# The second MLP product by Strassen's scheme, in two passes, with two blocks' norms under the second pass

## Chip, cores and metric

The program runs on one core of one Trainium2 chip. The metric is the time of one execution in microseconds (us) on the device, the median of the runs made. An engine is named here by what it does: TensorE multiplies (PE in the rows; PEld is its loading of the stationary operand), VectorE is DVE, ScalarE is ACT, GpSimd is POOL, and SyncE (SP) issues most of the loads.

## What is computed

Two transformer-like blocks run one after the other on 512 tokens of width 1024, all in float32. The part around the change is the end of the first block and the start of the second:

```python
hn = rms_norm(x, norm2_w[l])
x = x + jnp.square(jax.nn.relu(hn @ mlp_w1[l])) @ mlp_w2[l]
...
return rms_norm(x, final_norm_w)
...
h = _rmsnorm(x, mix_norm_g[i])
z = h @ w_in[i]
u_f = z[..., :FOURIER_WIDTH]
u_s = z[..., FOURIER_WIDTH:FOURIER_WIDTH + SSM_WIDTH]
```

`mlp_w2` is 4096 x 1024. Behind it come a Fourier mix, a state-space mix, gates, an output product, a router and 64 experts with a hidden width of 512, whose weights are all read from HBM.

## The kernel before

Each engine has one program written out in order; semaphores join them. Tokens are four blocks of 128 (`i`). The eight PSUM banks of 512 columns are handed out by the helper `T` (class `Psum`): `full` counts a bank's finished tiles, `free` its emptied ones. `any_bank` hands the banks out in a ring. Weights go through four SBUF slots of 2 MB, `WR[0]` to `WR[3]`; the list `plan` says which weight takes which slot, and `load` in the program of SyncE waits, before it issues a transfer, until the last user of that slot is done. Transfers are issued strictly in the order of that program.

- The first MLP product (`mlp_in`) makes 32 tiles `("m1", m)` of 128 features by 512 tokens, eight matmuls each. ScalarE takes the ReLU (L1257), GpSimd squares (L2275), and the result is `HT`, 32 chunks `k` of 128 features by 512 tokens; semaphore `ht` counts them.
- Woven between these tiles stands the preparation of the state-space matrices in eight turns `c` (`ssm`): VectorE and GpSimd make outer products, TensorE transposes them (L664, L667) and multiplies small tiles (`zb`, L678, L684), ScalarE writes the results to DRAM (`mbr_d`, `mbi_d`, `mcr_d`, `mci_d`, `z_d`; semaphores `st0`, `st1`). On VectorE a table of powers (`Ep`, L1466 and L1869) follows.
- The second MLP product: `acc` holds 8 banks, block `i` by half `nh` of the 1024 outputs. In step `s_` one 2 MB piece of `m2` (four chunks `k`) is multiplied into all eight banks, 32 matmuls of 128x128 by 128x512 (L703; the profile counts two instructions for each float32 matmul). The last step goes bank by bank (L720).
- Behind it the residual is added (`add_m2`, L1882), the block gets its final norm (`final_norm`, L1887 and L1892, with ScalarE's squares L1069 and root L1319), then the norm of the second model (`mix_norm`, L1897, L1902, root L1327), TensorE transposes it (`mix_norm` on TensorE, L389), VectorE and ScalarE move it to `H` (`turn_out`, L1485, L1075), and `z2` (eight tiles, weights in two pieces) is multiplied, its first four tiles as two halves of 256 tokens (`half_tile`, L401), the others whole (`dense`, L382).
- `z2` tiles 0 to 3 go through DRAM (`u_d`) into `U` in another order; only then can TensorE start the state products `("v", ri, g8)` (L749, 64 columns each) with `mbr_d`, then `mbi_d`, read back. The Fourier tiles (L760), `yf` (L382), `within` (L778, needs `z_d` read back by L2448) and `borders` (L800, needs VectorE's scan: semaphore `sp`, four and then eight) follow. 
- Later the gates, the output product, the router and the experts follow; the experts' weights pass through nine slots.

## Time and profile before

| | |
|---|---|
| median of 3 runs | 2427.59 us (2423.2 to 2429.49) |
| span of the profiled execution | 2424.5 us |
| TensorE busy | 2204.2 us, 91% |
| TensorE's weight loading busy | 1011.7 us |
| VectorE, ScalarE, GpSimd busy | 607.9, 320.6, 212.6 us |
| mean granted TensorE clock | 0.972 of full speed |
| second MLP product, L703 and L720 | 835.12 to 1055.96 us |
| expert weights | from 1447.48 us on without a pause, about 425 GB/s |

The profiled execution has no time of its own beside its span; the span lies inside the range of the runs, 3.1 us under their median, so what a sum takes from the span is taken from the median too. An engine's share of busy time says nothing of one stage: a stage is read from its own rows. 1.00 of granted clock is 2.4 GHz, 0.50 is 1.2 GHz.

### The profile page before, as it was taken

How to read it: one execution, taken by the hardware profiler on the slowest of the kernel's cores; microseconds unless marked ns; L12 is line 12 of the kernel's file. 1: busy time of each engine (PE TensorE's matmuls, PEld its weight loads, DVE VectorE, ACT ScalarE, POOL GpSimd, SP SyncE). 2: the span in 40 equal slices, each digit the busy share in tenths (PEclk: the TensorE clock that was granted, in tenths of full speed). 3: DMA queues.
4: the chain of work that ended last, by engine and by line, in shares of the span. 5: the costliest groups of instructions: out<-in, count | busy, mean ns of one | idle time of the engine just before them, and what ended most of it. 6: DMA issues, size and time to landing. Idle time of an engine off the chain costs nothing.

```text
span 2424.5 us, 20330 instructions
## 1 busy us (share of the span) xinstructions
PE 2204.2 (91%) x8260; PEld 1011.7 (42%) x8260; DVE 607.9 (25%) x1295; ACT 320.6 (13%) x645; POOL 212.6 (9%) x192
## 2 busy tenths in 40 slices
PE   8999999999999999999999999978877888877776
PEld 5554444445444444466644463333322233322332
DVE  2146545301633220044621151110111111111114
ACT  2015324201111100021110120000000000000001
POOL 0001111010234200000000000000000000000001
PEclk9999999999999999998999999998999999999998
DMA  7201010321232321219523349999999999999995
GB/s 275 87 35 70 35 70 18 139 104 72 102 108 89 143 78 69 78 49 161 178 104 130 147 167 413 427 426 426 426 426 426 426 426 426 425 425 422 424 422 219
DMA packets 69759, 551.39 MB, mean 227 GB/s; under 512 B 21656, under 2 KB 26392, under 8 KB 37600
## 3 DMA queue, kind: packets, MB, share of 16 engines
q1 hardware_dynamic: 42384, 514.44, 52.2%
q10 hardware_dynamic: 17200, 23.23, 3.2%
q0 software_dynamic: 10080, 12.38, 1.5%
q8 instruction: 67, 1.10, 0.2%
q14 instruction: 28, 0.23, 0.0%
HBM read 542.86 MB, written 35.68 MB: 239 GB/s over the span
## 4 chain that ended last, share of the span: by engine, by line
PE 70%; DMA 25%; DVE 2%; ACT 1%; issue 1%; DVEq 0%; POOL 0%; ACTq 0%; SPq 0%; POOLq 0%
PE ps L382 25%; DMA sb<-in_eu 13%; DMA sb<-in_eg 9%; PE ps L1019 9%; PE ps L458 8%; PE ps L703 8%; PE ps L1051 4%; DMA sb<-in_ed 3%; PE ps L401 3%; PE ps L633 2%; PE ps L867 2%; PE ps L546 1%; PE ps L579 1%; PE ps L573 1%; PE ps L800 1%
## 5 line engine op out<-in xcount | busy, mean ns | idle before, releaser
L382 PE MATMUL ps<-sb 128*128 128x512 f32 (+2 forms) x1504 | 599.8, 558 | 2.3 <-issue 2.3
L1019 PE MATMUL ps<-sb 128*64 128x512 f32 x2048 | 487.0, 631 | 114.5 <-DMA sb<-in_eu 81.7
L382 PEld LDWEIGHTS ps<-sb 128*128 128x128 f32 x1504 | 273.7, 190 | 308.0 <-issue 304.7
L1019 PEld LDWEIGHTS ps<-sb 128*64 128x64 f32 x2048 | 175.6, 145 | 405.2 <-issue 405.1
L1051 PE MATMUL ps<-sb 128*64 128x512 f32 x992 | 227.8, 613 | 27.0 <-ACT sb L1442 17.3
L458 PE MATMUL ps<-sb 128*128 128x512 f32 x512 | 236.1, 600 | 0.1
L703 PE MATMUL ps<-sb 128*128 128x512 f32 x448 | 192.5, 592 | 0.7 <-ACT sb L1257 0.7
L1466 DVE TENSOR_TENSOR sb<-sb 128x512 f32<-128x512 f32 (+9 forms) x293 | 114.7, 410 | 114.3 <-PE ps L667 66.2
L1051 PEld LDWEIGHTS ps<-sb 128*64 128x64 f32 x992 | 73.3, 141 | 160.1 <-issue 135.4
L458 PEld LDWEIGHTS ps<-sb 128*128 128x128 f32 x512 | 91.2, 190 | 100.0 <-issue 98.2
L703 PEld LDWEIGHTS ps<-sb 128*128 128x128 f32 x448 | 85.0, 190 | 107.6 <-issue 107.6
L2360 POOL DMA_INDIRECT y_d<-sb x31 | 31.2, 1007 | 854.2 <-PE ps L1003 748.7
L2219 DVE SCALAR_TENSOR_TENSOR sb<-sb,ps 128x512 f32<-128x512 f32 x32 | 22.1, 690 | 301.8 <-PE ps L1019 301.8
L1081 ACT ACTIVATE sb<-ps 128x512 f32<-128x512 f32 (+3 forms) x100 | 52.8, 536 | 240.4 <-PE ps L382 77.7
L2214 DVE SCALAR_TENSOR_TENSOR sb<-sb,ps 128x512 f32<-128x512 f32 x32 | 22.1, 690 | 245.3 <-ACT sb L1438 245.3
L2264 POOL TENSOR_TENSOR sb<-sb 128x256 f32<-128x256 f32 (+3 forms) x32 | 41.6, 1300 | 371.0 <-DVE sb L1682 370.9
L1490 DVE COPY sb<-ps 128x512 f32<-128x512 f32 (+6 forms) x53 | 34.4, 650 | 145.7 <-PE ps L382 89.8
L1442 ACT ACTIVATE sb<-ps 128x512 f32<-128x512 f32 x32 | 19.2, 598 | 376.0 <-PE ps L1026 376.0
L401 PE MATMUL ps<-sb 128*128 128x256 f32 x256 | 61.7, 403 | 6.3 <-DVE sb L1485 3.5
L2209 DVE TENSOR_TENSOR sb<-ps,sb 128x512 f32<-128x512 f32 x64 | 41.4, 687 | 102.6 <-PE ps L1003 101.8
L2229 DVE COPY sb<-ps 128x512 f32<-128x512 f32 x31 | 21.5, 693 | 176.6 <-PE ps L1051 176.6
L867 PE MATMUL ps<-sb 128*128 128x512 f32 x128 | 58.4, 598 | 1.6 <-DVE sb L2008 1.6
(288 smaller groups left out, 1474.7 us busy)
## 6 DMA issues: line engine op xcount, KB each, us to landing
sb<-in_eg SPq DMA_DIRECT2D x64, 2048.0 KB, 32.8
sb<-in_eu SPq DMA_DIRECT2D x63, 2048.0 KB, 33.9
sb<-in_ed SPq DMA_DIRECT2D x63, 2048.0 KB, 33.0
sb<-in_m SPq DMA_DIRECT2D x16, 2048.0 KB, 7.3
sb<-in_mg SPq DMA_DIRECT2D x8, 1536.0 KB, 6.6
sb<-in_winF SPq DMA_DIRECT2D x5, 2048.0 KB, 7.3
sb<-in_mgg SPq DMA_DIRECT2D x4, 2048.0 KB, 7.9
sb<-in_wo SPq DMA_DIRECT2D x4, 2048.0 KB, 7.4
```

The source lines that it names most:

```text
L382: ins = pe.matmul(out, lhsT, rhs, start=k == 0, stop=k == len(pieces) - 1)
L401: ins = pe.matmul(T.ap(*tile)[:, t], lhsT, rhs[:, t], start=k == 0, stop=k == 7)
L458: ins = pe.matmul(o, lhsT, rhs, start=k == 0, stop=k == 7)
L633: ins = pe.matmul(o, MG1[:, k, 128 * i:128 * i + 128], wo[nh][:, k, :], start=k == 0, stop=k == 7)
L703: ins = pe.matmul(acc[2 * i + nh], HT[:, k, 128 * i:128 * i + 128], w[:, q, 512 * nh:512 * nh + 512], start=k == 0, stop=False)
L867: ins = pe.matmul(T.ap(*name), MG2[:, k, 128 * i:128 * i + 128], wo[nh][:, k, :], start=k == 0, stop=k == 7)
L1019: ins = pe.matmul(o[64 * e:64 * e + 64, :], x[:, k, 64 * e:64 * e + 64], weight(2 * mat + e)[:, 512 * k:512 * k + 512], start=k == 0, stop ...
L1051: ins = pe.matmul(o[64 * e:64 * e + 64, :], aT[:, k, 64 * e:64 * e + 64], weight(4 + e)[:, d:d + 512], start=k == 0, stop=k == 3)
L1081: act.activation(dst, T.ap(*name) if src is None else src, ACT.Copy).then_inc(T.s(*name), 1)
L1466: return own(dve.tensor_tensor(o, a, b, op))
L2209: dve.tensor_tensor(XT[:, 4 * hf:4 * hf + 4, :], table.ap("xt", q, hf).rearrange("p (a b) -> p a b", a=4), bc(ck("gx")[:, 4 * hf:4 * hf + ...
L2264: pool.tensor_tensor(pr, pr, bc(ST[u % 4][:, 2:4], 2, nk), ALU.mult).then_inc(S("prob"), 1)
```

## The change

The product by `m2` is done in two passes (`turn`), each for two token blocks. In a pass, a step takes the same 2 MB piece as before, seen as 2 x 2 blocks (pairs of feature chunks, even and odd, by halves of the outputs), and one level of Strassen's scheme in Winograd's form makes seven products of two matmuls each where the plain scheme for two token blocks has eight. So `m2` is read twice: 16 loads in place of 8. VectorE makes four sums of weights (`t`, 1024 elements per partition) and four of activations (`a`, 256 elements) per step (`block_sums`), double-buffered in `TW` and `SW`: the first step's weight sums lie where the table `Ep` comes later, those of odd steps in `WR[3]`, those of even steps in `H`. Seven banks accumulate the products `f`; the eighth (`bank_t`) holds transposes. At the end of a pass `block_results` combines the seven products with the residual.

The norms of blocks 0 and 1 stand in VectorE's and ScalarE's programs between the sums of the second pass, and their transposes stand on TensorE between the products of step 15. The table of powers is a generator whose pieces stand between the sums of steps 2 to 6. The last `zb` tile stands ahead of the last `m1` tile. Of `z2` five tiles, not four, are done as halves. Its pieces take other slots, so that `mbr_d` and `mbi_d` are read back after `z2` at earlier places.

```diff
+        TW = [view(zone, 20480, 4, 2, 512), view(WR[3], 0, 4, 2, 512)]
+        TW += [shaped(H.rearrange("p a b -> p (a b)"), 8, 512).rearrange("p (a c) b -> p a c b", c=2)]
+        SW = [[view(zone, 2048 + 1024 * q, 8, 128) for q in range(2)], [HT[:, 8 * q:8 * q + 8, 0:128] for q in range(2)]]
+        UW = [[view(zone, 512 * q, 2, 256) for q in range(3)], [HT[:, 16 + 2 * q:18 + 2 * q, 0:256] for q in range(3)]]
...
-        plan += [(("m1", g), (0, 2, 1)[g % 3]) for g in range(8)] + [(("m2", g), g % 3) for g in range(8)]
-        plan += [(("z2", 0), 3), (("z2", 1), 0), (("dft", 0), 1), (("mbr", 0), 3), (("mbi", 0), 0), (("z", 0), 3),
+        plan += [(("m1", g), (0, 2, 1)[g % 3]) for g in range(8)] + [(("m2", g), (1, 0, 2)[g % 3]) for g in range(16)]
+        plan += [(("z2", 0), 0), (("z2", 1), 2), (("dft", 0), 1), (("mbr", 0), 3), (("mbi", 0), 0), (("z", 0), 3),
...
+        def step_done(n):
+            return T.full("m2", n // 8, 6) if n % 8 == 7 else (S("m2w"), n + 1 - n // 8)
+
+        def sums_of(n):
+            t = TW[0] if n == 0 else TW[1] if n % 2 else TW[2]
+            s_ = SW[n // 8][n % 2]
+            return [t[:, q] for q in range(4)], [s_[:, 2 * q:2 * q + 2, :] for q in range(4)]
...
+            base = ring[0]
+            bank_t = (base + 7) % 8
+            for n in range(16):
+                turn, s_ = n // 8, n % 8
+                tsum, ssum = sums_of(n)
+                w = view(slot("m2", n), 0, 2, 2, 2, 512)
+                lo, hi = slice(256 * turn, 256 * turn + 128), slice(256 * turn + 128, 256 * turn + 256)
+                pe.wait_ge(*loaded("m2", n))
+                if turn == 0:
+                    pe.wait_ge(S("ht"), 4 * s_ + 4)
+                even, odd = [4 * s_, 4 * s_ + 2], [4 * s_ + 1, 4 * s_ + 3]
+                factors = [
+                    ([HT[:, k, lo] for k in even], [w[:, j, 0, 0] for j in range(2)]),
+                    ([HT[:, k, lo] for k in odd], [w[:, j, 1, 0] for j in range(2)]),
+                    ([ssum[1][:, j] for j in range(2)], [tsum[1][:, j] for j in range(2)]),
+                    ([ssum[2][:, j] for j in range(2)], [tsum[2][:, j] for j in range(2)]),
+                    ([ssum[0][:, j] for j in range(2)], [tsum[0][:, j] for j in range(2)]),
+                    ([ssum[3][:, j] for j in range(2)], [w[:, j, 1, 1] for j in range(2)]),
+                    ([HT[:, k, hi] for k in odd], [tsum[3][:, j] for j in range(2)]),
+                ]
+                for f, (a, b) in enumerate(factors):
+                    if s_ == 0:
+                        open_tile(pe, ("m2", turn, f), (base + f) % 8)
+                    if f == 2:
+                        pe.wait_ge(S("m2s"), n + 1)
+                    for j in range(2):
+                        ins = pe.matmul(T.ap("m2", turn, f), a[j], b[j], start=s_ == 0 and j == 0, stop=s_ == 7 and j == 1)
+                    if s_ == 7:
+                        ins.then_inc(T.f("m2", turn, f), 1)
+                    elif f == 6:
+                        ins.then_inc(S("m2w"), 1)
+                    if n == 15 and f in (0, 2, 3, 5):
+                        i, h = divmod((0, 2, 3, 5).index(f), 2)
+                        pe.wait_ge(S("xn"), 4 + i + 1)
+                        turned_half(2, i, h, XN, bank_t)
+                W.ended[("m2", n)] = n
...
+            half_tile(2, ("z2", 0), "z2", 0, 0, bank_t)
+            half_tile(2, ("z2", 1), "z2", 1, 0, base % 8)
+            half_tile(2, ("z2", 2), "z2", 2, 0, (base + 1) % 8)
+            mix_norm(2, 3)
+            half_tile(2, ("z2", 3), "z2", 3, 0, (base + 2) % 8)
+            mix_norm(3, 5)
+            pe.wait_ge(*loaded("z2", 1))
+            half_tile(2, ("z2", 4), "z2", 4, 0, (base + 3) % 8)
+            for m in range(5):
                 half_tile(2, ("z2", m), "z2", m, 1)
-            for m in range(4, 8):
+            ring[0] = base + 4
+            for m in range(5, 8):
                 dense(("z2", m), "z2", m, any_bank())
...
+            first_product(0)
             sums(0)
-            root_a(0)
-            sum_b(0)
             sums(1)
-            root_b(0)
-            root_a(1)
-            sum_b(1)
+            for i in range(2):
+                root_a(i)
+                sum_b(i)
+            for i in range(2):
+                root_b(i)
+            first_product(1)
+            turn_out(2, 0, sm("mix"))
+            turn_out(2, 1, sm("mix"))
...
-                        yield
+                        if c < 7 or way:
+                            yield
...
+                    if q == 5:
+                        yield
...
+            def block_sums(n):
+                turn, s_ = n // 8, n % 8
+                t, a = sums_of(n)
+                w = view(slot("m2", n), 0, 2, 2, 2, 512)
+                b11, b12, b21, b22 = w[:, :, 0, 0], w[:, :, 0, 1], w[:, :, 1, 0], w[:, :, 1, 1]
+                lo, hi = slice(256 * turn, 256 * turn + 128), slice(256 * turn + 128, 256 * turn + 256)
+                h = HT[:, 4 * s_:4 * s_ + 4, :].rearrange("p (j q) b -> p j q b", q=2)
+                a11, a12, a21, a22 = h[:, :, 0, lo], h[:, :, 1, lo], h[:, :, 0, hi], h[:, :, 1, hi]
+                dve.wait_ge(*loaded("m2", n))
+                if n == 0:
+                    dve.wait_ge(*T.full("mb", 7, 1))
+                elif n == 1:
+                    dve.wait_ge(S("st0"), 512)
+                    dve.wait_ge(S("st1"), 512)
+                elif n == 2:
+                    dve.wait_ge(*T.full("m1", 31))
+                    dve.wait_ge(*step_done(0))
                 else:
-                    after(own(ins))
-                    cmul(pw2[q % 2], pw, pw)
-                    pw = pw2[q % 2]
-
-
-            def add_m2(i):
-                for nh in range(2):
-                    xs = X[:, i, 512 * nh:512 * nh + 512]
-                    dve.wait_ge(*T.full("m2", i, nh))
-                    dve.scalar_tensor_tensor(xs, T.ap("m2", i, nh), norm_r[1][:, i:i + 1], xs, ALU.mult, ALU.add).then_inc(T.s("m2", i, nh), 1)
+                    dve.wait_ge(*step_done(n - 2))
+                if turn == 0:
+                    dve.wait_ge(S("ht"), 4 * s_ + 4)
+                t1 = tt(t[0], b12, b11, ALU.subtract)
+                if n == 0:
+                    dve.wait_ge(*T.full("zb", 7, 1))
+                s1 = tt(a[0], a21, a22, ALU.add)
+                after(t1)
+                t2 = tt(t[1], b22, t[0], ALU.subtract)
+                after(s1)
+                s2 = tt(a[1], a[0], a11, ALU.subtract)
+                tt(t[2], b22, b12, ALU.subtract)
+                tt(a[2], a11, a21, ALU.subtract)
+                after(t2)
+                tt(t[3], b21, t[1], ALU.subtract)
+                after(s2)
+                dve.tensor_tensor(a[3], a12, a[1], ALU.subtract).then_inc(S("m2s"), 1)
...
+                dve.wait_ge(*T.free("m2", turn, 0))
+                after(own(add(x00, r0, p1)))
+                add(x00, r0, product(1)).then_inc(T.s("m2", turn, 1), 1)
+                dve.tensor_tensor(u2, product(2), p1, ALU.add).then_inc(T.s("m2", turn, 2), 1)
+                dve.wait_ge(*T.free("m2", turn, 2))
+                x01_u2 = own(add(x01, r0, u2))
+                dve.tensor_tensor(u3, product(3), u2, ALU.add).then_inc(T.s("m2", turn, 3), 1)
+                yield
+                dve.wait_ge(*T.free("m2", turn, 3))
+                x10_u3 = own(add(x10, r1, u3))
+                x11_u3 = own(add(x11, r1, u3))
+                after(x01_u2)
+                x01_p5 = own(add(x01, r0, product(4)))
+                after(x11_u3)
+                add(x11, r1, product(4)).then_inc(T.s("m2", turn, 4), 1)
+                after(x01_p5)
+                add(x01, r0, product(5)).then_inc(T.s("m2", turn, 5), 1)
+                after(x10_u3)
+                add(x10, r1, product(6)).then_inc(T.s("m2", turn, 6), 1)
...
+            for n in range(9):
+                block_sums(n)
+                if 2 <= n < 7:
+                    next(ep_steps, None)
+            for _ in ep_steps:
+                pass
+            for _ in block_results(0):
+                pass
...
+            block_sums(9)
+            for i in range(2):
+                block_sums(10 + i)
+                final_norm(i)
+            for i in range(2):
+                block_sums(12 + i)
+                mix_norm(i)
+            block_sums(14)
+            block_sums(15)
             turn_out(2, 0, sm("mix"))
+            results = block_results(1)
+            next(results)
+            turn_out(2, 1, sm("mix"))
+            for _ in results:
+                pass
             final_norm(2)
-            add_m2(3)
+            final_norm(3)
...
+            pool.wait_ge(*step_done(0))
...
-            for g in range(8):
-                load(("m2", g), A["m2"][:, 4096 * g:4096 * g + 4096])
-            sp.wait_ge(S("mg1"), 8)
-            sp.wait_ge(S("st0"), 512)
-            sp.wait_ge(S("st1"), 512)
+            for n in range(16):
+                load(("m2", n), A["m2"][:, 4096 * (n % 8):4096 * (n % 8) + 4096])
             for g in range(2):
                 fours("z2", g, 8)
             load(("dft", 0), A["dft"], 2048)
+            sp.wait_ge(S("st0"), 512)
+            sp.wait_ge(S("st1"), 512)
+            sp.wait_ge(*step_done(15))
```

How the order of instructions changes on TensorE at the start of the second product (bank semaphores `free`, `ht` of the activations, `m2s` of the sums, `w` of a slot's load). Before, the last small tiles of `ssm` (L678) stand between the last `m1` tile (L382) and the product, whose first instruction waits for all eight banks:

```order
L382 MATMUL ps<-sb 128x512 [waits free2]
L382 MATMUL ps<-sb 128x512 x7
L678 MATMUL ps<-sb 16x128 [waits free3]
L678 MATMUL ps<-sb 16x128 x7
L703 MATMUL ps<-sb 128x512 [waits free5,free6,free4,free7,free3,w0,free2,ht,free1,free0]
L703 MATMUL ps<-sb 128x512 x7
L703 MATMUL ps<-sb 128x512 [waits ht]
```

and now (L396 is the `m1` tile, L738 the new product):

```order
L698 MATMUL ps<-sb 16x128 [waits free2]
L698 MATMUL ps<-sb 16x128 x7
L396 MATMUL ps<-sb 128x512 [waits free3]
L396 MATMUL ps<-sb 128x512 x7
L738 MATMUL ps<-sb 128x512 [waits free4,ht,w1]
L738 MATMUL ps<-sb 128x512
L738 MATMUL ps<-sb 128x512 [waits free5]
L738 MATMUL ps<-sb 128x512
L738 MATMUL ps<-sb 128x512 [waits m2s,free6]
```

The product starts on one bank that was emptied long ago, and the first thing in a step that needs VectorE's sums is its fifth matmul.

On TensorE at the end of the product, before (L389 are transposes of normed blocks, semaphore `xn`; L401 the halves of `z2`):

```order
L389 MATMUL ps<-sb 128x128 [waits free2,xn]
L389 MATMUL ps<-sb 128x128 x3
L389 MATMUL ps<-sb 128x128 [waits free3]
L389 MATMUL ps<-sb 128x128 x3
L401 MATMUL ps<-sb 128x256 [waits free1,free2,free0,free3,w3]
L401 MATMUL ps<-sb 128x256 x7
L389 MATMUL ps<-sb 128x128 [waits free4,xn]
```

and now, from the last product of step 15 on (L410 are transposes, L421 the halves of `z2`):

```order
L738 MATMUL ps<-sb 128x512 x2
L421 MATMUL ps<-sb 128x256 [waits free3,w0]
L421 MATMUL ps<-sb 128x256 x7
L421 MATMUL ps<-sb 128x256 [waits free3,free4]
L421 MATMUL ps<-sb 128x256 x7
L421 MATMUL ps<-sb 128x256 [waits free3,free5]
L421 MATMUL ps<-sb 128x256 x7
L410 MATMUL ps<-sb 128x128 [waits free7,xn]
L410 MATMUL ps<-sb 128x128 x3
```

Three halves of `z2` now stand between the end of the product and the transposes of block 2, and one more ahead of those of block 3; before, the first half of `z2` waited for blocks 0 and 1 and stood right behind their transposes.

On VectorE behind the last turn of `ssm`, before, the powers come first:

```order
L1466 TENSOR_TENSOR sb<-sb 128x32 [waits ep_one,mcm]
L1466 TENSOR_TENSOR sb<-sb 128x32
L1466 TENSOR_TENSOR sb<-sb 128x32 [waits dve]
L1466 TENSOR_TENSOR sb<-sb 128x32
L1466 TENSOR_TENSOR sb<-sb 128x32 [waits dve]
```

and now the eight sums of step 0 stand there, then those of steps 1 and 2, before the powers begin:

```order
L1499 TENSOR_TENSOR sb<-sb 128x1024 [waits full7,ht,w1,mcm]
L1499 TENSOR_TENSOR sb<-sb 128x256 [waits full2]
L1499 TENSOR_TENSOR sb<-sb 128x1024 [waits dve]
L1499 TENSOR_TENSOR sb<-sb 128x256 [waits dve]
L1499 TENSOR_TENSOR sb<-sb 128x1024
L1499 TENSOR_TENSOR sb<-sb 128x256
L1499 TENSOR_TENSOR sb<-sb 128x1024 [waits dve]
L1951 TENSOR_TENSOR sb<-sb 128x256 [waits dve]
L1499 TENSOR_TENSOR sb<-sb 128x1024 [waits st1,ht,st0,w0]
```

`full2` is the last `zb` tile, which reads what the first activation sum overwrites.

## Rows read from the trace of the kernel before

**Rows 1.** The page: busy time, share of the span, instructions

```profile
PE 2204.2 (91%) x8260; PEld 1011.7 (42%) x8260; DVE 607.9 (25%) x1295; ACT 320.6 (13%) x645; POOL 212.6 (9%) x192
```

**Rows 2.** Timeline of TensorE: start, length, what, [idle before <- what ended it]

```profile
607.70 48.23 PE L382 MATMUL ps<-sb 128*128 128x512 f32 x112
...
835.12 192.50 PE L703 MATMUL ps<-sb 128*128 128x512 f32 x448 [0.66 <-ACT sb L1257]
1027.46 20.76 PE L720 MATMUL ps<-sb 128*128 128x512 f32 x48
...
1060.35 6.55 PE L401 MATMUL ps<-sb 128*128 128x256 f32 x16 [3.51 <-DVE sb L1485]
...
1075.39 17.43 PE L401 MATMUL ps<-sb 128*128 128x256 f32 x80
...
1120.13 7.25 PE L749 MATMUL ps<-sb 128*128 128x64 f32 x64
1128.41 11.58 PE L749 MATMUL ps<-sb 128*128 128x64 f32 x64 [1.03 <-DMA sb<-mbi_d]
1139.79 3.73 PE L760 MATMUL ps<-sb 128*128 128x128 f32 x16
...
1144.98 2.05 PE L760 MATMUL ps<-sb 128*128 128x128 f32 x16
...
1154.92 3.68 PE L778 MATMUL ps<-sb 128*128 128x64 f32 x32
...
1182.95 7.25 PE L800 MATMUL ps<-sb 128*128 128x64 f32 x64
```

**Rows 3.** Stretches: PE, PEld, DVE, ACT, POOL busy; PEclk, DMA share, GB/s

```profile
600.00:640.00 40.00, 40.00 (x113) 21.13 (x112) 30.40 (x127) 7.04 (x13) 6.27 (x6) 1.00 0.21 79
...
1060.00:1066.00 6.00, 5.65 (x13) 4.55 (x14) 2.30 (x8) 0.20 (x1) 0.00 (x0) 0.50 0.08 30
...
1120.00:1127.00 7.00, 7.00 (x64) 6.87 (x62) 3.99 (x6) 1.77 (x3) 5.57 (x4) 1.00 0.80 295
...
1131.00:1144.00 13.00, 13.00 (x62) 12.56 (x62) 10.67 (x11) 2.85 (x6) 0.29 (x2) 0.50 1.28 108
...
1450.00:2380.00 930.00, 760.04 (x3384) 290.83 (x3382) 108.31 (x179) 55.67 (x93) 60.73 (x60) 0.95 1.00 422
```

**Rows 4.** Timeline of VectorE

```profile
703.31 1.32 DVE L1466 TENSOR_TENSOR sb<-sb 128x512 f32<-128x512 f32 x1 [11.66 <-PE ps L667]
...
842.48 0.98 DVE L1466 TENSOR_TENSOR sb<-sb 128x32 f32<-128x32 f32 x5 [34.84 <-POOL sb L2309]
...
851.02 0.42 DVE L1869 TENSOR_TENSOR sb<-sb 128x256 f32<-128x256 f32 x1
...
863.08 1.23 DVE L1869 TENSOR_TENSOR sb<-sb 128x1024 f32<-128x1024 f32 x1
...
1036.07 0.21 DVE L1887 TENSOR_SCALAR sb<-sb 128x1 f32<-128x1 f32 x1 [0.79 <-ACT sb L1069]
...
1037.59 1.28 DVE L1892 SCALAR_TENSOR_TENSOR sb<-sb 128x1024 f32<-128x1024 f32 x1
...
1070.02 0.15 DVE L1897 TENSOR_SCALAR sb<-sb 128x1 f32<-128x1 f32 x1 [1.96 <-ACT sb L1069]
...
1071.48 0.75 DVE L1902 TENSOR_SCALAR sb<-sb 128x1024 f32<-128x1024 f32 x1
...
1176.97 1.21 DVE L1973 TENSOR_TENSOR sb<-sb 64x1008 f32<-64x1008 f32 x1
```

**Rows 5.** Transfers: issue on ScalarE's queue with its time, then counts, KB, us to landing

```profile
1104.07 5.57 ACTq L1363 DMA_DIRECT2D sb<-u_d  x8
...
sb<-in_m SPq DMA_DIRECT2D x16, 2048.0 KB, 7.3
...
sb<-z_d SPq DMA_DIRECT2D x8, 256.0 KB, 11.5
...
sb<-u_d ACTq DMA_DIRECT2D x8, 128.0 KB, 7.0
```

137 lines of the change are left out of this document (57 added, 80 removed).

## Prediction

> **What bounds the kernel now.** I read the page first: TensorE is busy for 91% of the span [rows 1]. Then its timeline around the change [rows 2], for its idle times and what ended them, and the same stretches with the granted clock [rows 3]. TensorE runs without a gap through the second product: 448 of its 512 instructions take 192.5 us, 0.430 each. Behind it stand two stalls. The first is 3.51 us ahead of the first `z2` half, which waits for the norms of the last blocks on VectorE. The second is 1.03 us in the state products, for `mbi_d`. Behind each the clock falls to 0.50: over 1060 to 1066, and over 1131 to 1144 [rows 3]. Later, from 1450 us on, the DMA share is 1.00 and the experts' weights set the pace [rows 3]. Their first buffers come free only through routing and the first experts, which stand behind all of this on TensorE; so what TensorE gains here moves the whole stream, and I count it in full.
>
> **What is removed.** (a) Strassen: 16 steps x 7 products x 2 matmuls = 224 matmuls against 256, so 64 of 512 instructions fewer, at 0.430: 27.5 us.
>
> (b) The product's first instruction waited 0.66 us for the bank of the last `m1` tile; now it takes a bank emptied earlier: 0.7 us.
>
> (c) The stall of 3.51 us ahead of `z2`, and the slow clock behind it. The first half tile took from 1060.35 to the transposes at about 1066.8, 6.4 us; five half tiles together took 17.43, 3.45 each from start to start [rows 2]. So 2.9 more, in all 6.4 us. The cover now: three halves of `z2`, 10.4 us, between the end of the product and block 2's transposes. VectorE must in that time add the last product (under 1 us), do the final norms of blocks 2 and 3 (from 1036.07 to 1038.87, 2.8 each) and the mix norm of block 2 (from 1070.02 to 1072.23, 2.2) [rows 4]: 8.6, and with the squares and roots of ScalarE that stand between them some 10, an estimate. Block 3's second norm has a further 1.0 (transposes) and 3.45, and needs 2.2 and two moves. Both fit with a few tenths to spare; I allow 0.5 for small waits.
>
> (d) `mbi_d` could be loaded only when the last `z2` tile was done. Now it takes the slot of the first piece of `z2` and starts after tile 3, more than 20 us earlier for a transfer of 8: the 1.03 us go. And the slow clock with them, I think: 64, 16, 8 and 16 instructions from 1128.41 to 1147.0 took 18.6 us; at the full clock 7.1 (as the 64 ahead of them) + 2.05 + 1.0 + 2.05 = 12.2 [rows 2], 6.4 less. In all 7.4 us.
>
> The clock term rests on this: the 64 state instructions at 1120 ran for 7 us with the clock at 1.00, and it fell only after the stall [rows 3]. "Activity releases the throttle" is how the Trainium skill has it (TensorE: Matmul & The Clock Gate, Part 1); by that rule (d) stands in full.
>
> **What is added, and what hides it.** (e) VectorE's sums, per step 4 of 1024 elements at 1.23 and 4 of 256 at 0.42: 6.6 us [rows 4]. TensorE's step lasts 28 x 0.430 = 12.0, and its first four matmuls, 3.4 us, need no sum. The sums of step n may start when step n-2 is done. The first piece of the powers (it ends ahead of the 128x256, so by 851.44) takes at most 9.0 from 842.48, all pieces 21.8 [rows 4]. So at the fullest place, counted from the end of step 0, the sums of step 2 end at 6.6, that piece at 15.6, the sums of step 3 at 22.2, and TensorE wants them at 24.0 + 3.4; five turns are 55 against 60. For step 0 the last `m1` tile (6.9 us) and the first four matmuls are the cover. Cost nothing; were there no cover, 105 us.
>
> (f) Does VectorE's traffic slow TensorE? At 607 to 655 us TensorE took 48.23 / 112 = 0.431 per instruction [rows 2], with VectorE 76% busy over 600 to 640 [rows 3]. Nothing; the bounds are 0 and 0.2% of 192 us.
>
> (g) Loads: 16 in place of 8, 7.3 us each [rows 5], one per 12.0 us. A load starts when its slot's step is done and its sums may start one step later, so 4.7 us are spare. Nothing.
>
> (h) `block_results(0)`: eleven operations of at most 0.75 behind the sums of step 8, done some 15 us after step 7 begins; the second pass wants bank `f` from 12.0 + 1.7 `f` on, and the banks come free in that order, bank 1 some 5 us ahead. Nothing. In step 15 the four transposes (no more of them than before) share one bank; each of its emptyings, about 1.1 us on ScalarE, lies under at least one product of 1.7.
>
> (i) Given back: TensorE arrives 7.4 us earlier, measured from the start of the state products, than two things that don't move with it. `z_d` is issued 7.25 us behind that start and moves 2.1 MB at the 108 GB/s of that stretch, 19.4 us [rows 3]: there at 26.7, while TensorE now wants it at 34.8 - 7.4 = 27.4 (1154.92 less 1120.13). It just fits. VectorE's scan ended at 1178.18 and was wanted at 1182.95 [rows 2, 4], 4.8 us spare; it starts behind a state tile that itself comes about 2 us earlier, so 4.8 + 2 - 7.4 = -0.6. I take 0.9 for both.
>
> Sum: 27.5 + 0.7 + 6.4 + 7.4 - 0.5 - 0.9 = 40.6 us. From the span, 2424.5 - 40.6 = 2383.9; as the median stands 3.1 above, 2387.0.
>
> **The rivals.**
> 1. The clock falls in the state products all the same. For it: their tiles are 64 columns wide, and at 1131 to 1144 it stayed low although TensorE never idled; it rose only with the wider work. Against it: the 7 us at 1.00 ahead [rows 3]. Another road to the same end: `U` comes late. Its eight reads were issued by 1109.6 and land in 7.0, by 1116.6; that is 23.8 us behind the end of `z2` tile 3 (1092.8). The cover was 27.3 and is now one half and three whole tiles, 3.45 + 3 x 6.9 = 24.1: 0.3 us spare by that bound. Then (d) is 1.0 and (i) is nothing: 27.5 + 0.7 + 6.4 + 1.0 - 0.5 = 35.1, 2392.5. Chance 0.25.
> 2. The norms come late after all, TensorE waits again ahead of block 2's transposes, and the clock falls behind it. (c) is lost and a stall of up to 3.5 may stand in its place: 34.2 less, 2393.4; with rival 1, 2399. For it: the margin is under 1 us on an estimate of ScalarE's share. Chance 0.11.
> 3. On the other side: VectorE's sums become the bound. For it: an addition of 512 elements took 1.32 us with GpSimd beside it [rows 4], twice as much per element as the 1024 in 1.23. If strided operands in four dimensions cost the same without GpSimd, a step is 13.3, above 12.0, and the powers come on top: 16 x 1.3 + 22 = 43 us lost, 2430. It decides from 12.0 + 40.6 / 16 = 14.5 us a step. Against it: GpSimd stands idle here but for the last squares. Chance 0.03. The Trainium skill (SBUF — State Buffer, SBUF: two separate sides) makes that 1.32 an exclusive lock on a port pair that only VectorE and GpSimd share; by that rule only the sums of step 0 can double, and the sum stays as it is.
> 4. Switching banks costs time: seven banks in turn, each tile of two matmuls, and TensorE idles a little at every change until the clock drops. At the half clock the product would take up to 192 us more, some 2579. Against it: the old product changes its bank at every matmul and still keeps 0.430 [rows 2]. Chance 0.01. The rule is the Trainium skill's (TensorE: Matmul & The Clock Gate, A second HAM failure mode: psum-queue depth-cycling).
> 5. The experts' stream doesn't move, because something other than TensorE's path opens it: 2427.6. Nothing in the rows names such a thing. Chance 0.02.
>
> **How the numbers follow.** My forecast has 0.58; its own range is 2383 to 2391 (waits in (c) and (i) between 0 and 4). The likeliest is 2387.0. Rivals 1 and 2 reach to 2399; the range 2381 to 2397 leaves out their joint case and the others. A difference of 0.3% (7.3 us) is about what measurements of this kernel can tell. Faster: 0.58 + 0.25 + 0.11 = 0.94; within 0.3%: rival 5 and a hundredth of rival 3, which ends near the old time, 0.03; slower: the rest of rival 3 and rival 4, 0.03.
>
> **What would show it.** The product from its first to its last matmul near 192.4 us plus 2 of transposes, with no idle time above a few tenths inside, VectorE busy for about 6.6 us in every 12. No wait ahead of `z2` above 0.5, no clock of 0.50 there. `mbi_d` issued right behind tile 3 of `z2`; 128 state instructions in 14.5 us. If the clock falls there, rival 1. If `m2s` ends waits in the product, rival 3. A wait of TensorE for `xn`, rival 2. What would make all of it wrong is an expert stream that starts no earlier.

## The result, and the profile after

| | before | changed |
|---|---|---|
| median of 4 runs each | 2428.54 us (2423.20 to 2433.60) | 2393.62 us (2388.03 to 2406.47) |
| ratio | | 0.9872, 95% interval 0.9854 to 0.9891 |
| span of the profiled execution | 2424.5 us | 2386.2 us |
| VectorE busy | 607.9 us | 712.7 us |

The changed kernel is 1.3% faster; I had forecast 2387.0. By the ratio it stands at 2397.5 where before stands at 2428.5, and 2397.5 is also the median of the 16 executions made of it on three occasions. They lie between 2386 and 2409, twice as far apart as those of the kernel before (2422 to 2434), and where that spread comes from is half of the story. (The ratio is not that of the two medians alone; where a text below compares two kernels "by the ratios", it compares each one's ratio to the kernel before.)

The page of the changed kernel, the line that answers to [rows 1]:

```profile
PE 2179.7 (91%) x8212; PEld 998.7 (42%) x8212; DVE 712.7 (30%) x1437; ACT 321.8 (13%) x647; POOL 216.8 (9%) x192
```

Its timeline of TensorE (start, length, line, tile, idle time before it and what ended that), from the product to `borders`. L738 is the product, L410 transposes, L421 the halves of `z2`, L396 whole tiles, L776 the state products, L787 and L793 the Fourier tiles, L805 `within`, L827 `borders`; it answers to [rows 2]:

```profile
830.79 182.13 PE L738 MATMUL ps<-sb 128*128 128x512 f32 x424
...
1024.81 10.52 PE L421 MATMUL ps<-sb 128*128 128x256 f32 x48
1035.17 1.04 PE L410 MATMUL ps<-sb 128*128 128x128 f32 x8
...
1061.10 20.76 PE L396 MATMUL ps<-sb 128*128 128x512 f32 x48
1081.70 14.43 PE L776 MATMUL ps<-sb 128*128 128x64 f32 x128
1095.96 2.00 PE L787 MATMUL ps<-sb 128*128 128x128 f32 x16
...
1101.86 7.11 PE L396 MATMUL ps<-sb 128*128 128x512 f32 x16 [0.95 <-issue]
1112.42 7.09 PE L805 MATMUL ps<-sb 128*128 128x64 f32 x32 [3.45 <-DMA sb<-z_d]
1119.30 4.96 PE L396 MATMUL ps<-sb 128*128 128x512 f32 x8
1124.10 3.68 PE L805 MATMUL ps<-sb 128*128 128x64 f32 x32
1127.62 3.65 PE L396 MATMUL ps<-sb 128*128 128x512 f32 x8
...
1145.12 7.25 PE L827 MATMUL ps<-sb 128*128 128x64 f32 x64
```

Three things are to be seen. The product has no idle time, nor has anything behind it for 270 us: the stalls of 3.51 and 1.03 us of [rows 2] are gone. All 128 state instructions run in 14.43 us, at the full clock. And a new stall stands ahead of `within`: 3.45 us for `z_d`, which before was there in time. Behind it 32 instructions take 7.09 us, where the next 32 take 3.68, and 8 take 4.96, where the next 8 take 3.65. So the half clock costs 3.4 + 1.3 = 4.7 more.

The windows of this kernel (PE, PEld, DVE, ACT, POOL busy; PEclk, DMA share, GB/s), the answer to [rows 3]:

```profile
843.00:883.00 40.00, 40.00 (x94) 17.68 (x93) 34.92 (x79) 0.00 (x0) 0.21 (x2) 1.00 0.49 184
1025.00:1035.00 10.00, 10.00 (x48) 8.79 (x48) 6.76 (x22) 4.57 (x14) 0.00 (x0) 1.00 0.81 315
1083.00:1097.00 14.00, 14.00 (x127) 14.00 (x127) 8.56 (x12) 4.73 (x8) 5.41 (x4) 1.00 0.57 55
1113.00:1121.00 8.00, 8.00 (x33) 7.08 (x33) 7.87 (x8) 0.00 (x0) 0.00 (x0) 0.50 0.36 146
```

VectorE, the neighbour of [rows 4] here, has a step's seven sums of L1499 and the eighth of L1951 in 6.0 us, and the norms of the last blocks just ahead of the transposes at 1035.17 and 1039.50:

```profile
843.17 5.63 DVE L1499 TENSOR_TENSOR sb<-sb 128x1024 f32<-128x1024 f32 x7 [8.29 <-PE ps L738]
848.73 0.42 DVE L1951 TENSOR_TENSOR sb<-sb 128x256 f32<-128x256 f32 x1
...
1033.54 0.75 DVE L2013 TENSOR_SCALAR sb<-sb 128x1024 f32<-128x1024 f32 x1
...
1038.55 0.75 DVE L2013 TENSOR_SCALAR sb<-sb 128x1024 f32<-128x1024 f32 x1
```

The useful balance is by stage. From the first instruction of the product to the second `borders` it was 1182.95 - 835.12 = 347.8 us, and is 1145.12 - 830.79 = 314.3: 33.5 less. From there to the end of the span it was 1241.6 and is 1241.1 (1240.3 to 1243.2 in all thirteen traces of this case), so whatever TensorE gains here the whole kernel gains. Of the 4.3 us ahead of the product some 0.8 belong to the change: the wait of 0.66 us for the last `m1` bank, term (b), is gone. The rest lies in code that the change does not touch: 1.7 us net at the start, where 16 matmuls at 14 us took 3.69 us here and 5.71 before, and 1.7 us at 532 us, where 40 matmuls took 17.43 and 19.11.

### The profile page after: what moved, and what is told of

Read it like the earlier page. It is cut to its first block, busy times and chain, and to the rows that moved or that the text cites. A ratio compares the mean times of both kernels' runs of the same rounds, so it can differ in the third digit from the quotient of the medians.

```text
span 2386.2 us, 20426 instructions
## 1 busy us (share of the span) xinstructions
PE 2179.7 (91%) x8212; PEld 998.7 (42%) x8212; DVE 712.7 (30%) x1437; ACT 321.8 (13%) x647; POOL 216.8 (9%) x192
## 4 chain that ended last, share of the span: by engine, by line
PE 70%; DMA 25%; DVE 2%; ACT 1%; issue 1%; SPq 0%; DVEq 0%; POOL 0%; ACTq 0%; POOLq 0%
PE ps L396 24%; DMA sb<-in_eu 13%; PE ps L1046 9%; PE ps L478 9%; PE ps L738 8%; DMA sb<-in_eg 7%; DMA sb<-in_ed 5%; PE ps L1078 4%; PE ps L421 3%; PE ps L894 2%; PE ps L653 2%; PE ps L566 1%; PE ps L599 1%; PE ps L593 1%; DMA sb<-z_d 1%
## 5 line engine op out<-in xcount | busy, mean ns | idle before, releaser
L396 PE MATMUL ps<-sb 128*128 128x512 f32 (+2 forms) x1488 | 594.3, 559 | 2.3 <-issue 2.3
L1046 PE MATMUL ps<-sb 128*64 128x512 f32 x2048 | 483.2, 627 | 97.6 <-DMA sb<-in_eu 70.3
L396 PEld LDWEIGHTS ps<-sb 128*128 128x128 f32 x1488 | 271.4, 191 | 304.9 <-issue 301.7
L1078 PE MATMUL ps<-sb 128*64 128x512 f32 x992 | 243.6, 648 | 32.1 <-DMA sb<-in_ed 16.9
L1499 DVE TENSOR_TENSOR sb<-sb 128x256 f32<-128x256 f32 (+8 forms) x405 | 205.8, 540 | 145.5 <-PE ps L687 77.9
L478 PE MATMUL ps<-sb 128*128 128x512 f32 x512 | 236.1, 600 | 0.0
L738 PE MATMUL ps<-sb 128*128 128x512 f32 x448 | 193.1, 592 | 0.0
L738 PEld LDWEIGHTS ps<-sb 128*128 128x128 f32 x448 | 84.9, 190 | 105.2 <-issue 105.2
L421 PE MATMUL ps<-sb 128*128 128x256 f32 x288 | 63.6, 380 | 3.0 <-ACT sb L1102 3.0
L1502 DVE TENSOR_SCALAR sb<-sb 128x512 f32<-128x512 f32 (+6 forms) x116 | 33.0, 284 | 103.9 <-ACT sb L1193 32.3
```

Of the source, the lines that this page charges most:

```text
L396: ins = pe.matmul(out, lhsT, rhs, start=k == 0, stop=k == len(pieces) - 1)
L421: ins = pe.matmul(T.ap(*tile)[:, t], lhsT, rhs[:, t], start=k == 0, stop=k == 7)
L478: ins = pe.matmul(o, lhsT, rhs, start=k == 0, stop=k == 7)
L738: ins = pe.matmul(T.ap("m2", turn, f), a[j], b[j], start=s_ == 0 and j == 0, stop=s_ == 7 and j == 1)
L1046: ins = pe.matmul(o[64 * e:64 * e + 64, :], x[:, k, 64 * e:64 * e + 64], weight(2 * mat + e)[:, 512 * k:512 * k + 512], start=k == 0, stop ...
L1078: ins = pe.matmul(o[64 * e:64 * e + 64, :], aT[:, k, 64 * e:64 * e + 64], weight(4 + e)[:, d:d + 512], start=k == 0, stop=k == 3)
```

## The experiments

In each, the stretch from the first instruction of the product to the second `borders` (the "stretch" below) is read beside the median.

**The changed kernel again.** No edit; it gives a second trace and the level on this chip.

> The changed kernel once more, for a firmer size. My reading of its first trace: in the stage itself it gains 34 us (27.5 for the matmuls, 0.7, 6.4 and 7.4 for the stalls and the slow clock behind them, less 8.2 for a new wait for z_d with a slow clock behind it); the 3.6 us that the trace gained before the change's first instruction are luck. So a ratio of 0.986 (0.985 to 0.988). If the experts' stage lost something too, 0.989 or more.

Measured: 2398.62 us (2390.52 to 2409.28, 6 runs), ratio 0.9891 (0.9867 to 0.9915). That lies above the 0.985 to 0.988 that I expected, at the value I had given for a loss in the experts' stage; the trace shows none (1242.6 us behind the stretch, where the other traces have 1240.3 to 1243.2), and the stretch is 313.8 us. So the loss is in executions that this trace does not show. This execution shows a second stall that the first did not have, ahead of the state products, with no slow clock behind it; the engine is put down to "issue", but what the instruction waits for here is `U`:

```profile
1084.61 14.48 PE L776 MATMUL ps<-sb 128*128 128x64 f32 x128 [1.24 <-issue]
...
1114.61 5.34 PE L805 MATMUL ps<-sb 128*128 128x64 f32 x32 [2.68 <-DMA sb<-z_d]
```

**`within` behind the Fourier tiles.** The wait for `z_d` is put off by two Fourier tiles:

```diff
-                if g == 2:
-                    pe.wait_ge(*loaded("z", 0))
-                for g8 in ((), (), (0, 1), (2, 3))[g]:
-                    within(g8)
...
+            pe.wait_ge(*loaded("z", 0))
+            for g8 in range(4):
+                last = within(g8)
+            last.then_inc(S("z_used"), 1)
```

and SyncE waits for `z_used` before it loads the next weight into that slot.

> The changed kernel, with the four groups of `within` (which need z_d) behind the four Fourier tiles instead of between them, so that z_d is wanted 6.9 us later. Theory: the wait of 3.45 us for z_d and the 4.7 us of slow clock behind it go, and 0.6 come back as a wait for VectorE's scan: 7.5 us under the changed kernel, ratio to the kernel before 0.983. Rival, that z_d only happens to be late in this one trace and is no usual cost: no difference to the changed kernel. Rival, that the small tiles in one piece (four groups of 32, 14 us) pull the clock down by themselves: the wait is gone and the clock falls nevertheless, a gain of 3 to 4.

Measured: 2398.29 us (2385.77 to 2400.32, 6 runs), ratio 0.9877 (0.9854 to 0.9900). In the trace the stall and the slow clock behind it are gone, with 0.63 us of waiting for VectorE's scan in their place, and the stretch is 306.8 us, 7.5 under the first trace. The median did not follow: I expected 0.983. So `z_d` is real, and something else moves the executions by as much. One such thing stands in this very trace. The product began at 842.08 us, 11.3 later than in the first one, mostly because 64 small matmuls far ahead of the change ran at half speed behind a short stall (7.33 us for the same 64 in the first trace):

```profile
108.02 12.88 PE L396 MATMUL ps<-sb 128*128 128x62 f32 x64 [1.38 <-issue]
```

It is no effect of this edit, as the last experiments show, and it can't be all, as four of the six executions are longer still (2398 to 2400 against this one's 2393.0).

**The kernel before with the `z2` pieces in slots 0 and 2.** This is the one part of the change that frees `mbi_d`:

```diff
-        plan += [(("z2", 0), 3), (("z2", 1), 0), (("dft", 0), 1), ...
+        plan += [(("z2", 0), 0), (("z2", 1), 2), (("dft", 0), 1), ...
```

> The kernel before, with one edit: the two pieces of z2 take slots 0 and 2 as in the change, so that mbi_d is loaded behind tile 3 of z2. Theory: the 1.0 us stall for mbi_d and the slow clock behind it go (7.4 us) and the wait for z_d with its slow clock comes (3.3 + 4.7): the same time as before, within 2 us. By the step of my prediction as it stood, 6.5 us faster. If the small tiles pull the clock down by themselves, the clock still falls in the state products and the time is 1 us less.

Measured: 2428.0 us (12 runs), ratio 1.0008 (0.9992 to 1.0024). Its timeline (L749 state products, L778 `within`, L382 whole tiles):

```profile
1118.61 14.40 PE L749 MATMUL ps<-sb 128*128 128x64 f32 x128
...
1148.53 6.99 PE L778 MATMUL ps<-sb 128*128 128x64 f32 x32 [2.68 <-DMA sb<-z_d]
1155.31 5.44 PE L382 MATMUL ps<-sb 128*128 128x512 f32 x8
```

The stall for `mbi_d` and its slow clock go, as my term (d) had it, and about the same amount comes back at `z_d` (2.68 us of stall and 5.1 of slow clock): the stretch is 346.7 us against 347.8. That is the failure of term (i) in small, without Strassen's scheme.

**The same, with `within` behind the Fourier tiles.** Both edits on the kernel before.

> The kernel before with both edits, the slots of z2 and `within` behind the Fourier tiles. Theory: both stalls and both stretches of slow clock are gone, 7.4 less 0.6 for the scan: 6.8 us under the kernel before, ratio 0.997. If the small tiles pull the clock down by themselves, 1 us or nothing.

Measured: 2425.11 us (12 runs), ratio 0.9985 (0.9971 to 0.9999), in two clusters, 2416 to 2420 and 2424 to 2426. The stretch is 340.9 us, 6.9 less than before, as expected. The trace gives the gain in full; the ratio gives half of it (3.6 us), the medians 1.1. The traced execution (2419.4) is one of the lower cluster, and its 64 matmuls at 107 us ran at full speed; that the upper cluster has them slow is likely by the 7 us between the two, but no trace shows it.

**Eight products' worth of multiplication.** The seventh product is multiplied twice into its bank, which leaves sums, banks, loads and order alone (the numbers that come out are then not the reference's):

```diff
-                    for j in range(2):
+                    js = (0, 1, 0, 1) if f == 6 else (0, 1)
+                    for c, j in enumerate(js):
```

> The changed kernel, but in each of the 16 steps the seventh product is multiplied twice into its bank, so that a pass does the eight products' worth of matmuls that the plain scheme has (512 instructions instead of 448); the output is then not the reference's. It leaves the sums, the banks, the loads and the order as they are, and so prices the saved multiplication alone. My theory (TensorE's saved time comes through in full): 16 x 2 matmuls x 0.86 = 27.5 us slower than the changed kernel of the same chip, the product 209.6 us long without a gap. Rival (part of the saving is lost further on, in waits that only an earlier TensorE meets): the sums and loads get 13.7 instead of 12.0 us a step here, so were they a hidden brake in the changed kernel, the difference would be below 20 us. The waits behind z2 are measured from the end of z2 and should not alter.

Measured: 2426.58 us (2417.76 to 2436.64, 10 runs), ratio 1.0009 (0.9993 to 1.0025), all the gain gone. The changed kernel was not run beside it; by the ratios this one is 29 to 33 us slower. In the timeline (L739 is the product here) the piece of 424 instructions is now 484, still without idle time, and the first half of `z2` starts 221.49 us after the product does, where it was 194.02:

```profile
832.86 207.88 PE L739 MATMUL ps<-sb 128*128 128x512 f32 x484
...
1054.35 10.52 PE L421 MATMUL ps<-sb 128*128 128x256 f32 x48
```

The difference is 27.47 us against the 27.5 expected, and 28.0 over the whole stretch (342.3 against 314.3): what the seven products save comes through, and the rival (below 20) is out.

**`U` ahead of `mbi_d`.** SyncE waits, before it loads `mbi_d`, until `U` is back:

```diff
+            sp.wait_ge(S("u2"), 128)
```

> The changed kernel with one wait more on SyncE: the load of mbi_d is issued only when U has been read back, so that the 1 MB write of u_d and its reads no longer share the DMA engines with a 2 MB load. In the changed kernel the write takes 11.4 us to land with that load issued 0.8 us ahead of it; with the way free I expect about 5 to 7, so U is there some 5 us earlier, well before TensorE wants it at the end of z2. mbi_d is then issued about 6 us later than now and lands in 6 to 8, which is still ahead of the 7.2 us of the mbr_d tiles or at most 1 to 2 us behind. If U's lateness is what makes some executions of the changed kernel longer (they lie at 2390, 2399 and 2409, about 8 us apart), the long ones go and the median falls by about 5 to 8 us, to 2391. Rival: the executions differ by where the clock falls elsewhere, and the median stays within 2 us of the changed kernel's.

Measured: 2391.98 us (2387.85 to 2397.63, 4 runs), ratio 0.9861 (0.9836 to 0.9886), 2 to 7 us under the changed kernel by the ratios, within what four runs can tell, and no execution above 2398. I expected about 2391. ScalarE's queue shows what the edit does. In the changed kernel the reads of `U` are issued 11.4 us behind the write of `u_d`:

```profile
1058.64 0.38 ACTq L1392 DMA_DIRECT2D u_d<-sb  x1
1070.08 5.26 ACTq L1396 DMA_DIRECT2D sb<-u_d  x8
```

and here 4.4 us behind it:

```profile
1060.20 0.38 ACTq L1392 DMA_DIRECT2D u_d<-sb  x1
1064.56 7.09 ACTq L1396 DMA_DIRECT2D sb<-u_d  x8
```

So what made the write slow is the 2 MB load of `mbi_d`, which the changed kernel issues 0.8 us ahead of it (SyncE's queue of that kernel, then its transfers with KB and us to landing):

```profile
1057.84 0.33 SPq L2515 DMA_DIRECT2D sb<-mbi_d  x1
1089.01 11.43 SPq L2562 DMA_DIRECT2D sb<-z_d  x8
```

```profile
sb<-mbi_d SPq DMA_DIRECT2D x1, 2048.0 KB, 9.2
...
u_d<-sb ACTq DMA_DIRECT2D x1, 1024.0 KB, 11.4
```

The Trainium skill (DMA: Bandwidth & Descriptors, Queues, rings and completion order) says that each DMA engine takes turns between the queues that have work, a packet at a time; the trace agrees that the two share, but the write landed at 1070.0, after the load at 1067.0.

Such a neighbour is not new, though. In the kernel before, the load of `mbr_d` stood there, 0.8 us ahead of the write, which then took 10.4 us to the reads at 1104.07 [rows 5]:

```profile
1092.86 0.33 SPq L2401 DMA_DIRECT2D sb<-mbr_d  x1
1093.66 0.38 ACTq L1359 DMA_DIRECT2D u_d<-sb  x1
```

`z_d` is still waited for here, for 5.03 us; the stretch is 316.8. It was issued as long after the start of the state products as in the changed kernel (7.3 us), when `mbi_d` had landed, and TensorE could start 25.0 us after its first issue instead of 23.4. Whether this edit makes it slower is open: the same time lies between 22.6 and 25.0 in the five traces that wait for `z_d`.

**Both edits on the changed kernel.**

> The kernel of the run before it with the tiles of within behind all four Fourier tiles as well, so that z_d has 7.8 us longer to come; neither z_d nor U is then waited for. From the trace of the changed kernel the stall of 3.45 and the 4.7 us of slow clock behind it go and the wait for the scan comes in for about 0.6 to 1 us: 7 us less in an execution like that one, 2386 to 2389. Rival: as the same edit on the changed kernel alone gave no difference of the medians (2398.3 against 2398.6), something behind it takes the gain back, and this one too stays near 2398.

Measured: 2385.52 us (2381.64 to 2393.83, 5 runs), ratio 0.9836 (0.9813 to 0.9860). The stretch is 306.8 us, with no wait but 1.04 us of issue and 0.54 us for the scan. It went past my 2386 to 2389 by a little, and the rival (2398) is out. The traced execution, 2390.7 us, is one of the two long ones: its 64 matmuls at 108 us took 12.85 us, and the product began at 841.77.

**The norms behind the product.** The sums of steps 9 to 15 stand together on VectorE, and then:

```diff
+            dve.wait_ge(*T.full("m2", 1, 6))
+            for i in range(2):
+                final_norm(i)
+            for i in range(2):
+                mix_norm(i)
```

with the four transposes on TensorE behind the product.

> The changed kernel without the part that puts the first two blocks' norms under the second pass: VectorE does them only when the last product of step 15 is full, and their transposes stand on TensorE behind the product instead of between the products of step 15. VectorE then has, with TensorE waiting, two final norms and two mix norms, 2.8 and 2.2 us each, and ScalarE's squares and roots between them: a stall of 12 to 16 us ahead of the first half of z2. Block 2's and 3's sums of products and norms, 7 + 10 us, start only then, against 10.4 us of z2 halves: another 5 to 9 us. With the half clock behind each, 20 to 30 us slower than the changed kernel, so about all that the seven products save. Rival: block 2's and 3's work can be overlapped and only the first stall counts, 12 to 16 us slower.

Measured: 2417.65 us (2406.47 to 2422.07, 10 runs), ratio 0.9958 (0.9942 to 0.9974), 16 to 21 us over the changed kernel by the ratios. The timeline:

```profile
1036.82 1.11 PE L410 MATMUL ps<-sb 128*128 128x128 f32 x4 [9.63 <-DVE sb L2013]
1039.54 1.11 PE L410 MATMUL ps<-sb 128*128 128x128 f32 x4 [1.61 <-DVE sb L1518]
...
1046.29 12.20 PE L421 MATMUL ps<-sb 128*128 128x256 f32 x48 [1.32 <-ACT sb L1102]
1107.22 27.23 PE L776 MATMUL ps<-sb 128*128 128x64 f32 x128 [2.05 <-issue]
1134.25 3.73 PE L787 MATMUL ps<-sb 128*128 128x128 f32 x16
```

The first stalls are 14.7 us together (9.63 + 1.61 + 1.32 + 0.78 + 1.32, two of them in the rows left out), as expected; the second set of 5 to 9 us did not come, so that half of my expectation was wrong. What was not expected stands at 1107: `U` is 2.05 us late, and behind that wait the 128 state instructions run at half speed (all but the first few), 27.23 us instead of 14.4. The stretch is 342.3 us, 27.9 more than in the first trace.

**`U` later by one write.** To see whether `U` makes the long executions, its write is done twice, in a row:

```diff
             act.wait_ge(S("u"), 16)
+            act.dma_start(u_d.rearrange("(m p) t -> p m t", p=P), usT).then_inc(S("u"), 16)
+            act.wait_ge(S("u"), 32)
```

> The changed kernel with the 1 MB write of u_d done twice, one after the other, before U is read back: U is late by one more write, 4.3 us to land with nothing beside it (the kernel with U first showed that) and 0.4 to issue. My theory is that the long executions of the changed kernel are those in which U comes late and the clock falls behind that stall, as in the kernel with the norms behind the product: 2.05 us of wait there, then 27.2 us for the 128 state instructions instead of 14.4. So here nearly every execution should have it: a stall of 4 to 6 us, 12.8 us more for the state products, 2 for the Fourier tiles; given back are the 8.1 us at z_d, which is no longer waited for, less 0.9. Together some 12 us more than an execution of the changed kernel with U in time: median 2406 to 2412 against 2398. Rival: the stall by itself does not bring the clock down, and the median is within 3 us of the changed kernel's, as z_d's stall gives way to U's.

Measured: 2403.48 us (2401.41 to 2413.07, 6 runs), ratio 0.9909 (0.9888 to 0.9930). This is 2.5 us below the lower end of what I expected, but outside the rival too (5.4 over the changed kernel on the same chip by the medians, 9 by the ratios, though the two intervals just overlap). The trace has the mechanism, 3.57 us of wait and 27.54 us of state products, and then `within` without a wait; the stretch is 324.0 us, 9.7 more than in the first trace:

```profile
1096.73 27.54 PE L776 MATMUL ps<-sb 128*128 128x64 f32 x128 [3.57 <-issue]
```

The lowest execution rose from 2386 to 2401. The traced one, 2410.8 us, again has the slow matmuls at 108 us on top (12.74 us, product from 842.09); that the four below 2404 have `U` alone is likely, but they have no trace.

**The changed kernel and the one with both edits, side by side.** No new edits; same chip as the run above.

> The changed kernel once more, for runs on the same chip as the other two, and for another look at where one of its executions loses time. Median 2394 to 2399; the trace should have a wait for z_d of about 3 us with the half clock behind it, U between 0 and 2 us late, and the state products in 14.4 us or, where U is late, perhaps in 27.

> The changed kernel with both edits (mbi_d loaded only when U is back, within behind the four Fourier tiles) again, on the same chip as the changed kernel. If both waits are what the changed kernel still loses, the median is 2383 to 2388, 10 to 13 us under the changed kernel's, and no execution is above 2396. Rival: the 2385.5 of the first time was luck of few runs, and the two are within 5 us.

Measured: the changed kernel 2398.11 us (2386.05 to 2407.70, 6 runs), ratio 0.9871 (0.9846 to 0.9895); with both edits 2384.81 us (2383.97 to 2385.61, 5 runs), ratio 0.9826 (0.9808 to 0.9844). This time the profiler caught a long execution of the changed kernel, 2405.9 us:

```profile
104.69 1.88 PE L478 MATMUL ps<-sb 128*128 128x512 f32 x4
107.96 12.67 PE L396 MATMUL ps<-sb 128*128 128x62 f32 x64 [1.39 <-issue]
...
1094.81 26.69 PE L776 MATMUL ps<-sb 128*128 128x64 f32 x128 [1.73 <-issue]
1121.30 3.73 PE L787 MATMUL ps<-sb 128*128 128x128 f32 x16
1124.95 1.76 PE L793 MATMUL ps<-sb 128*1 128x128 f32 x8
...
1136.59 3.68 PE L805 MATMUL ps<-sb 128*128 128x64 f32 x32
```

Its windows show the clock at 0.50 in the state products (it fell within their first microsecond) and back at 1.00 afterwards, when `z_d` is in time:

```profile
1096.00:1120.00 24.00, 24.00 (x114) 24.00 (x114) 8.63 (x10) 4.14 (x7) 3.63 (x4) 0.50 0.55 50
1138.00:1146.00 8.00, 8.00 (x52) 6.09 (x51) 7.86 (x8) 0.60 (x1) 0.29 (x2) 1.00 0.01 2
```

The kernel with both edits, 2383.8 us (here L828 is `borders`):

```profile
107.56 7.33 PE L396 MATMUL ps<-sb 128*128 128x62 f32 x64 [1.38 <-issue]
...
1086.31 14.40 PE L776 MATMUL ps<-sb 128*128 128x64 f32 x128
...
1106.44 13.97 PE L396 MATMUL ps<-sb 128*128 128x512 f32 x32 [0.95 <-issue]
1120.25 7.25 PE L805 MATMUL ps<-sb 128*128 128x64 f32 x64
...
1142.20 7.36 PE L828 MATMUL ps<-sb 128*128 128x64 f32 x64 [0.63 <-DVE sb L2090]
```

The 2405.9 are then accounted for. The stretch is 322.6 us, 8.3 more than in the first trace: 1.7 of wait, 12.3 in the state products, 1.7 and 0.7 in the Fourier tiles, less 8.2 at `z_d`. The product itself began at 842.02 instead of 830.79, 11.2 later, all of it in code that the change doesn't touch. 3.0 were lost at the very start (16 matmuls at 14 us took 6.70 us instead of 3.69). 6.6 were lost at 108 us, where 64 small matmuls ran at half speed behind a stall of 1.39 us, and the 12 behind them began slow. The rest was lost at 541 us (40 matmuls in 19.13 instead of 17.43). The kernel with both edits had the same stall, 1.38 us, and no slow clock behind it. Of the thirteen traces of this case, four have the slow matmuls at 108 us; in these four the product begins between 841.8 and 842.1, in the other nine between 830.8 and 835.4.

## Why the prediction was wrong

Step by step, by the letters of the prediction:

- **(a) Right.** 27.47 us for the 64 instructions, by the run that puts them back.
- **(b), (c) Right.** No wait ahead of the product or of `z2` (the first is worth some 0.8 us, ahead of the stretch), and the clock at 1.00 over 1025 to 1035. The norms are ready 0.9 us (block 2) and 0.2 us (block 3) ahead of their transposes; the few tenths I gave were the margin, and the 0.5 allowed for small waits were not needed. Their place under the second pass matters: moved behind the product they cost 16 to 21 us, and part of that by `U` and the clock.
- **(d) Right where `U` is in time:** 14.43 us for 128 instructions against the 14.5 forecast, and the same in the kernel before with the slots alone. What brought the clock down in these traces was a stall, not the narrow tiles. The Trainium skill's rule, that activity releases the throttle (TensorE: Matmul & The Clock Gate, Part 1), held as far as I used it; but where the clock had fallen, TensorE was busy without a pause from 1096 to 1120 us and the clock stayed at 0.50, and there the trace differs from it.
- **(e) to (h) Right.** Sums 6.0 us a step (I had 6.6), VectorE busy for 34.9 of 40 us behind the first step, where it is fullest, and TensorE still at 182.13 / 424 = 0.430 us. The Trainium skill (TensorE: Matmul & The Clock Gate, A second HAM failure mode: psum-queue depth-cycling) reports a kernel whose change of banks in every iteration let TensorE idle a little and the clock swing; here, with seven banks in turn, there was no idle time, and the clock was 1.00 throughout.
- **(i) This step failed.** I had "It just fits" and 0.9 us; it cost 3.45 of stall + 4.7 of slow clock, 8.2 (in the second trace 2.7 + 3.5 = 6.1). Two errors made it. I took the arrival of `z_d` from bytes and rate alone, 19.4 us after the first issue; it took 1112.42 - 1089.01 = 23.4. The trace of before had the better number: its eight reads of `z_d` were issued from 1127.4 to 1134.7 and took up to 15.1 us each to land, so they were there by 1149.8, at most 22.4 us after the first issue and some 5 us before `within` wanted them, where TensorE was to come 7.4 earlier. And I priced the wait by its length, though the terms (c) and (d) rest on a stall costing its slow clock as well. With 8.2 in place of 0.9, and without (b), which lies ahead of it, my sum for the stretch is 32.6 us, and the trace shows 33.5; half a microsecond of the difference is the allowance for small waits that was not needed.
- **Rival 1, second road: the place was right, the price was not.** I wrote that `U` had 0.3 us to spare "by that bound" and gave the case 0.25, worth 5.5 us. In three traces of the changed kernel it was 0, 1.24 and 1.73 us late, and in the last the state products ran at half speed but for their first microsecond: 16.4 us lost (1.7 + 12.3 + 2.4), of which the 8.2 at `z_d` come back, so that its stretch is only 25.2 us shorter than before. I had valued it by the stall in the old kernel, which stood between the two halves of the state products and so slowed only what was left of them. `U`'s margin went in two parts. From the write of `u_d` to the place where TensorE wants `U` it was 1120.13 - 1093.66 = 26.5 us and is 1081.70 - 1058.64 = 23.1; this I had counted. The write then took 11.1 to 11.4 us beside the load of `mbi_d`, where it had taken 10.4 beside that of `mbr_d`, and this alone is more than the 0.3 us that I had left. Whether `U` is late then hangs on its reads: their median time to landing was 6.0 us in the first trace, in time, and 6.9 and 7.2 us in the two in which it was late. That the write suffered from a large load beside it at all, before as well, I had not seen; it is worth 7 us.

That the two late transfers were all that was missing in the stretch is shown by the kernel without them: 306.8 us in both its traces, 41.0 less than before, where the sum without (b) said 39.9. Its medians are 2384.8 on a chip where before was at 2426.3, 41.5 less, and 2385.5 where before was at 2424.7, 39.1 less; the forecast was 40.6. The mechanism of the change was understood; what it does to two transfers downstream was not.

Open stays how often `U` is late enough. The 16 executions of the changed kernel spread evenly from 2386 to 2409; three of them have a trace. That the thirteen without one differ by `U` and by the slow stretch at 108 us is argued from those three, from the floor of 2401 with `U` delayed and from the kernel with both mended. That kernel ran from 2384.0 to 2385.6 on one occasion, but from 2381.6 to 2393.8 on the other, where the trace of the 2390.7 has the slow stretch at 108 us. So the narrow range is in part luck: mending `U` and `z_d` does not touch that part, and it is not the change's. The kernel before most likely has it too, as its executions stand mainly at 2422 to 2430 with a group at 2434, but its trace was taken without it. The median of `within` moved alone (2398.3) also fits, as where `U` is late and `z_d` therefore in time it mends nothing, but no trace of such an execution was taken.

## What to carry to other kernels

When a change lets the bounding engine arrive earlier, list every transfer that doesn't move with it, take its time from first issue to the waiting instruction in a trace of the same transfer (not from bytes and rate), and price each near miss as the stall plus the slow clock over all that stands behind it. A small transfer on the critical path that starts right behind a large load is worth keeping apart from it. A median that ignores a gain the trace plainly shows points to a second cause of the same size: look at a long execution, not only at the fastest, and read when the changed stage starts as well as how long it lasts.

## What the hardware showed beyond that

A stall's length alone did not decide whether the clock fell. In the state products, 1.24 us of wait left it at 1.00, and 1.73, 2.05 and 3.57 us brought 0.50 for all 128 instructions or all but the first few; but in the kernel before, 1.03 us of wait was followed by 0.50 too, from 1131 us on [rows 3]. At 108 us the same stall of 1.38 to 1.39 us was followed by 64 instructions in 7.33 us in nine traces and in 12.67 to 12.88 us in four. What differed ahead of them was the start: the nine began between 104.93 and 107.56 us, the four between 107.74 and 108.04, and that lateness came from the first 16 matmuls at 14 us, which took 3.69 to 6.38 us in the nine and 6.47 to 6.70 in the four. Whether the start decides, and why it should, no run here shows. The Trainium skill (TensorE: Matmul & The Clock Gate, Part 1) says that the gate's watching runs freely, so that the cost varies from run to run; these rows agree that it varies, and here it moved one kernel by 6.6 us at that place alone. And once down, the clock stayed down over some 26 us of 64-column matmuls without idle time, while 14.4 us of the same work held 1.00 when it came in at 1.00.

A 1 MB write took 4.3 us to land with nothing beside it and 10.4 to 11.6 us with a 2 MB load issued 0.8 us ahead of it.
